# Modulation's sum over partitions: block transposes and row sums on VectorE and four small matmuls in place of 16 TensorE transposes

## The reference

```
mod = silu(c) @ w_mod + b_mod                 # 2048 -> 6 x 2048
sh1, sc1, g1, sh2, sc2, g2 = split(mod, 6)
h = rmsnorm(x, g) * (1 + sc1) + sh1 ; x = x + g1 * attention(h)
h = rmsnorm(x, g) * (1 + sc2) + sh2 ; x = x + g2 * ffn(h)
```

## Time and profile before

| | |
|---|---|
| median of 3 runs | 2319.56 us (2314.96 to 2319.98) |
| profiled execution | 2319.4 us, of which the span from first to last instruction is 2317.5 |
| TensorE, VectorE, ScalarE, GpSimd busy | 2222.8, 1506.3, 1005.4, 15.5 us |
| mean granted TensorE clock | 0.983 of full speed |
| the six sums: transposes (L1507), 96 | 13.2 us busy |
| reductions (L893), 12 | 14.1 us busy |

### The profile page before, as it was taken

One profiled execution on the slowest core, in us unless ns is written; L12 is line 12 of the kernel. 1 busy time (PEld: TensorE's weight loads), 2 busy tenths in 40 slices (PEclk: granted clock), 3 DMA queues, 4 the chain that ended last, 5 costly groups with the idle time before them and its releaser, 6 DMA issues.

```text
span 2317.5 us, 29464 instructions
## 1 busy us (share of the span) xinstructions
PE 2222.8 (96%) x11498; PEld 1901.7 (82%) x11498; DVE 1506.3 (65%) x1417; ACT 1005.4 (43%) x1249; POOL 15.5 (1%) x39
## 2 busy tenths in 40 slices
PE   7999989999999999999999798999999999999997
PEld 6888778788888888888878697787888888888886
DVE  6666455787677767777777864557555655655655
ACT  5443163544344334334354543535443443443442
POOL 0000000000000000000000000000000000000000
PEclk9999999999999999999999899999999999999999
DMA  8775505867877877878867263155656556656553
GB/s 317 285 283 168 162 1 222 283 230 294 290 277 261 307 264 258 310 254 290 294 231 290 91 200 124 74 199 146 194 188 197 185 188 195 189 193 186 181 199 125
DMA packets 213106, 499.67 MB, mean 216 GB/s; under 512 B 10068, under 2 KB 12680, under 8 KB 199800
## 3 DMA queue, kind: packets, MB, share of 16 engines
q1 hardware_dynamic: 211528, 491.16, 61.9%
q0 software_dynamic: 1456, 6.72, 0.8%
HBM read 495.68 MB, written 2.17 MB: 215 GB/s over the span
## 4 chain that ended last, share of the span: by engine, by line
PE 58%; issue 36%; DVE 3%; ACT 1%; DMA 1%; SPq 0%; POOL 0%; DVEq 0%; ACTq 0%; POOLq 0%
PE ps L1443 17%; PE ps L1432 9%; PE ps L1433 9%; PE ps L1434 9%; PE ps L1448 9%; PE ps L1612 2%; ACT prob L665 1%; PE ps L1490 1%; PE ps L1618 1%; DMA raw<-in_nsa_w_in_dram 1%; PE ps L1666 1%; DVE stat L1171 0%; PE ps L1543 0%; DVE h L1036 0%; PE ps L1507 0%
## 5 line engine op out<-in xcount | busy, mean ns | idle before, releaser
L866 DVE TENSOR_TENSOR lower<-raw,upper 128x1024 fp32r<-128x1024 f32 (+1 forms) x733 | 884.2, 1215 | 540.8 <-ACT upper L491 538.1
L491 ACT ACTIVATE upper<-raw 128x1024 fp32r<-128x1024 f32 (+1 forms) x733 | 769.8, 1055 | 974.1 <-PE ps L1434 540.7
L1443 PE MATMUL ps<-xs,upper 128*128 128x512 f32 x2688 | 677.4, 394 | 6.4 <-DVE h L956 4.5
L1443 PEld LDWEIGHTS ps<-xs,upper 128*128 128x128 f32 x2688 | 485.2, 190 | 95.7 <-issue 6.7
L1432 PE MATMUL ps<-upper,hidden 128*128 128x512 f32 x1024 | 399.2, 390 | 0.2 <-DVE lower L866 0.2
L1433 PE MATMUL ps<-lower,hidden 128*128 128x512 f32 x1024 | 398.5, 389 | 0.0
L1434 PE MATMUL ps<-upper,hidden 128*128 128x512 f32 x1024 | 398.4, 389 | 0.0
L1448 PEld LDWEIGHTS ps<-xs,lower 128*128 128x128 f32 x2688 | 367.5, 191 | 26.3
L1448 PE MATMUL ps<-xs,lower 128*128 128x256 f32 x2688 | 375.6, 283 | 0.0
L1432 PEld LDWEIGHTS ps<-upper,hidden 128*128 128x128 f32 x1024 | 192.2, 188 | 40.8 <-DVE lower L866 1.4
L1434 PEld LDWEIGHTS ps<-upper,hidden 128*128 128x128 f32 x1024 | 192.2, 188 | 40.4
(11 more groups left out here) (243 smaller groups left out, 1176.1 us busy)
## 6 DMA issues: line engine op xcount, KB each, us to landing
raw<-in_ffn_w_dram SPq DMA_DIRECT2D x128, 1024.0 KB, 5.9
raw<-in_w_ff_dram SPq DMA_DIRECT2D x128, 1024.0 KB, 5.3
modraw<-in_w_mod_dram SPq DMA_DIRECT2D x96, 1024.0 KB, 7.8
raw<-in_nsa_w_in_dram SPq DMA_DIRECT2D x40, 1024.0 KB, 5.2
raw<-in_nsa_w_out_dram SPq DMA_DIRECT2D x16, 1024.0 KB, 7.4
raw<-in_ple_w_gate_dram SPq DMA_DIRECT2D x16, 1024.0 KB, 5.2
raw<-in_w_out_dram SPq DMA_DIRECT2D x16, 1024.0 KB, 5.1
raw<-in_w_in_dram SPq DMA_DIRECT2D x12, 1024.0 KB, 5.3
```

Of the source, the lines that this page charges most:

```text
L491: nc.scalar.activation(dst, src, ACT.Copy).then_inc(upper_ready, 1)
L866: nc.vector.tensor_tensor(low, src, up, ALU.subtract).then_inc(lower_ready, 1)
L1443: mm(ps[:, 4 * par + f, :], up[:, kk, f * P:(f + 1) * P], both, start=(k == 0), stop=False, skip_group_check=True)
```

## The change

`fold_mod`, new, runs on VectorE: it transposes `modacc` in 32x32 blocks into `modfold` and sums every 32 columns, so that `modsum` [128, 64] holds at partition 32 r + j the sum over a quarter of the partitions. TensorE then adds the four quarters by four matmuls with `quads` (four 32x32 identities stacked, [128, 32]), each of 16 columns into 32 partitions of one bank. VectorE adds the bias from PSUM (16 columns). The order changes too: fold_mod stands at s = 3, TensorE's part behind step 5 instead of step 1, store_mod at s = 6 ahead of the second add_mod. The bias table's matmul stays behind step 1.

```diff
+            nc.gpsimd.memset(quads[:], 0.0)
...
+            for r in range(4):
+                sel = nc.gpsimd.affine_select(out=quads[:], in_=quads[:], compare_op=ALU.not_equal, fill=1.0,
+                                              base=-32 * r, pattern=[[-1, 32]], channel_multiplier=1)
+                if r < 3:
+                    link(sel)
...
+            def fold_mod():
+
+                dve.wait_ge(mod_added, c.at(mod_added))
+                link(nc.vector.transpose(modfold[:], modacc[:]))
+                nc.vector.tensor_reduce(modsum[:], modfold[:].rearrange("p (c i) -> p c i", i=32), AX.X,
+                                        ALU.add).then_inc(mod_folded, 1)
+
             def store_mod(m):
...
-                for i, bank in enumerate((2, 6)):
-                    op = nc.vector.tensor_reduce(modsum[:, i], ps[:, bank:bank + 2, :].rearrange("p b (k n) -> p (b k) n", n=P),
-                                                 AX.X, ALU.add)
-                link(op)
-                nc.vector.tensor_tensor(dst, modsum[:].rearrange("p a k -> p (a k)"), b, ALU.add).then_inc(mod_stored, 1)
+                nc.vector.tensor_tensor(dst, ps[:, 2, 0:KC], b, ALU.add).then_inc(mod_stored, 1)
...
                     if s == 3 and store is not None:
+                        fold_mod()
+                    if s == 6 and store is not None:
                         store_mod(store)
                     if mods is not None and s in at:
                         add_mod(mods + (s == at[1]))
...
+            fold_mod()
             store_mod(5)
...
-            def sum_mod(wait, before=-1):
-
-                pe.wait_ge(mod_added, wait)
+            def sum_mod(folded, before=-1):
+
+                pe.wait_ge(mod_folded, folded)
                 pe.wait_ge(evacuated, c.at("groups", before))
-                for k in range(KC):
-                    op = nc.tensor.transpose(ps[:, (2, 3, 6, 7)[k // 4], k % 4 * P:(k % 4 + 1) * P],
-                                             modacc[:, k * P:(k + 1) * P], ident[:])
+                for r in range(4):
+                    op = mm(ps[32 * r:32 * r + 32, 2, 0:KC], quads[:], modsum[:].rearrange("p (k r) -> p r k", r=4)[:, r, :],
+                            start=True, stop=True)
                 op.then_inc(mod_summed, 1)
...
-            def sums_and_bias():
-                sum_mod(KC)
-
+            def bias_by_bucket():
+                pe.wait_ge(evacuated, c.at("groups", -1))
                 pe.wait_ge(aux_landed, 16 * 5)
                 mm(ps[0:SWA_HEADS, 4, 0:P], relb[:], onehot[:], start=True, stop=True).then_inc(bias_sum, 1)
...
-            group(tokens, xs, between={1: sums_and_bias})
+            group(tokens, xs, between={1: bias_by_bucket, 5: lambda: sum_mod(1)})
...
-                    group(tokens, hidden, ready=ready, between={1: between} if between and g == 0 else None)
+                    group(tokens, hidden, ready=ready, between={5: between} if between and g == 0 else None)
```

More of the change, by code:

```diff
@@ L125, in program @@
         probT = place("probT", [P, 2, 12 * P], at=M + 12288)
+        modfold = place("modfold", [P, D], at=U + 32768)
         blk = place("blk", [P, CMP_LEN, NSA_G, N_CMP], at=G)
@@ L170, in program @@
         modcol = place("modcol", [P, 6, KC])
-        modsum = place("modsum", [P, 2, KC // 2])
+        modsum = place("modsum", [P, D // 32])
+        quads = place("quads", [P, 32])
         silu_c = place("silu_c", [P, KC])
@@ L204, in program @@
         mod_landed = [sem(f"mod_landed{i}") for i in range(2)]
-        mod_added, mod_summed, mod_stored = sem("mod_added"), sem("mod_summed"), sem("mod_stored")
+        mod_added, mod_folded, mod_summed, mod_stored = sem("mod_added"), sem("mod_folded"), sem("mod_summed"), sem("mod_stored")
         x_landed = [sem(f"x_landed{i}") for i in range(T)]
@@ L1728, in between @@
                     sum_mod(c.at("mods", 0))
-                    c.next("mods", KC)
+                    c.next("mods")
                 if modulated:
-                    c.n["mods"] = 2 * KC
+                    c.n["mods"] = 2
                 quarter(norms, between if modulated else None)
@@ L1734, in ffn @@
                 if modulated:
-                    per["mods"] = KC
+                    per["mods"] = 1
                 with loop(pe, c, QUARTERS - 1, per):
@@ L1752, in _ @@
             pe.wait_ge(evacuated, c.at("groups"))
-            sum_mod(6 * KC, 0)
+            sum_mod(6, 0)
             pe.wait_ge(mod_stored, 6)
```

## The result

The changed kernel takes 2328.52 us, the median of 6 runs (2324.51 to 2331.16), against 2319.77 for the kernel before (6 runs): a ratio of 1.0039, 95% interval 1.0027 to 1.0052. That is 8.75 us slower. The forecast was 14 us slower, with a range from 2321 to 2343. Of the eleven executions of a later kernel, the one with both orders, one took 7873.84 us and is left out of its ratio.

What follows compares the result with a forecast made beforehand. TensorE was taken as the bound where five of six sums are made. Terms: −1.2 first sum, +8.9 network, +3.9 last sum, +2.5 clock, together +14.1 us, giving 2333.5 us, range 2321 to 2343.

Steps and rivals of the forecast that it cites:

- the loop's three sums: Feed-forward loop's three trips: each sum costs 4.5 us in place of 1.75 + 0.4, +2.3 us each, +6.9 together.
- the last sum: At 1304 us, TensorE idle: fold, matmuls at half clock and store take 6.2 us in place of 2.35, +3.9 us.
- the clock term: Stalls of 2.2 us can lower TensorE's clock; one or two of four counted: +2.5 us, from nothing to +6.8.
- What TensorE saves: Per sum, 16 transposes costing 1.75 us give way to four matmuls costing 0.6: 1.15 us saved where nothing else moves.
- The nearest rows: Profile rows used to price TensorE's four new matmuls: at most 1.04 us for eight records, the middle, 0.5 us, taken.
- The fold's length: VectorE's block transpose and reduction at 2.35 us each: 4.7 us, or 4.74 with the semaphore between them.
- the 2.35 us row: Profile row of VectorE's second add, two tensors read; its pace was taken for both the transpose and the reduction.
- The 1.28 us row: Profile row of VectorE's first add, one tensor; the lower end for each new operation, making the fold 2.6 us.
- The first stall: TensorE waits ahead of step 4, since the fold runs ahead of split 4: 2.2 us, in the loop 2.3.
- The second stall: TensorE waits ahead of step 7: store_mod's wait at s = 6 holds up split 7, 1.0 us, in the loop 1.6.
- the late step 4: In the kernel before, step 4 of the loop's trips starts late behind a 0.21 us pause; counted as 0.4 us.
- The first sum: At 206 us: VectorE's earlier wait hides the fold and no add follows, so the saving stays, −1.2 us.

Runs made afterwards that it cites:

- both orders: Changed kernel with, in the feed-forward network, the fold behind split 4, the first add behind split 5 and store_mod behind split 7: 2314.14 us, ratio 0.9974 to the kernel before.
- the later store: Changed kernel with store_mod behind split 7 in the feed-forward network, instead of ahead of the second add and split 7: 2324.83 us, ratio 1.0023 to the kernel before.
- the early last fold: Changed kernel with the last section's fold ahead of the final norm, into a tile of its own: 2325.06 us, ratio 1.0028 to the kernel before.
- The kernels with 56 and 80 records: 56: the last section on TensorE, 2310.00 us. 80: both orders plus unused transposes, 16 in each of five sums (2329.21 us) or 48 in an idle stretch (2322.23 us).
- the last section on TensorE: Both orders, and for section 5 TensorE multiplies the unfolded sum with a column of ones instead of a fold: 2310.00 us, ratio 0.9960 to the kernel before.
- 48 transposes more: Both orders plus unused TensorE transposes: 16 in each of the first five sums, 2329.21 us, or 48 in the idle stretch at the first block's end, 2322.23 us.

## Why the prediction was right

The direction, the size to within its range, and both stalls in the network were right. The terms for the loop's three sums and for the last sum were too large, two were missing, and the clock term stood in the wrong place: that its size came out near the forecast is luck. The budget below splits the spans at the starts of the same ScalarE instructions (the 330th, 640th, 800th, 1000th and 1240th of 1249) and takes the means of two profiles of each kernel. The two profiles of the kernel before differ by 4.3 us in the first row and by up to 1.8 us in the others, so a row says no more than that.

| stretch | before | changed | difference |
|---|---|---|---|
| start to the first network, with the first sum | 470.2 | 469.0 | −1.2 |
| first network and embedding, four sums | 733.35 | 743.35 | +10.0 |
| gate's product to the second block's attention, last sum | 243.35 | 245.1 | +1.75 |
| attention and output | 250.1 | 250.0 | −0.1 |
| second network | 596.8 | 594.75 | −2.05 |
| rest | 24.55 | 25.1 | +0.55 |
| span | 2318.3 | 2327.3 | +9.0 |

- **What TensorE saves.** 1.75 us go, as read; putting them back cost 1.73. The four matmuls put off the next step by 0.28 us and slow the matmuls behind them by 0.15: 0.43 us where the forecast had 0.6. Their eight records stand within 0.26 us in the timeline. The nearest rows had a stationary of 128 columns, and I took half their price. The Trainium skill ("TensorEngine Tiling (Array Packing)", Tiling Modes and Performance Considerations) says that a stationary of 32 columns lets four column tiles of the array work at once; the trace agrees, with eight records of 0.2 us in 0.26 us.
- **The fold's length.** 4.63 us against 4.74 forecast. For the reduction the Trainium skill ("VectorE: DVE Perf Modes", the perf-mode tier table) lists the slowest mode even for fp32 from SBUF. The trace agrees: 2.29 us, the pace of the 2.35 us row. The 1.28 us row was the wrong neighbour for both operations.
- **The first stall.** Forecast 2.2 and 2.3 us, measured 2.12 from start to start (1.96 to 2.04 in the bracket). The two experiments that shorten or move the fold show its cause.
- **The second stall.** Forecast 1.0 and, in the loop, 1.6; measured pauses are 0.74 and 1.02, which from start to start are 0.16 more. The store's registers cost 0.3 us in the loop and not the 0.6 of the earlier trace rows.
- **A sum in the network.** Forecast +2.0 for the first and +2.3 for each trip. From its first matmul to the next group's first one, the group took 23.55, 24.13, 23.85 and 23.88 us before and takes 25.57, 25.89, 25.87 and 25.87 us: +2.0, +1.8, +2.0 and +2.0, 7.8 us in place of 8.9. The first was right. In the loop the second stall was 0.4 us too large, and of the kernel before I took the late step 4 of one trip for all three.
- **The first sum.** Its fold was hidden, as forecast. Its group took 24.09 us and takes 22.76, −1.3 us where −1.2 was forecast. Another 0.5 us went in the next group, where TensorE's wait for VectorE (tile `hid`, near 238 us) is 0.79 us in place of 1.29; no term had that.
- **The last sum.** Forecast +3.9, measured +2.7. The step that failed here is the price at half clock, 1.3 us for eight records and their latency. They took 0.31 us in all and the store began 0.37 us after their start.
- **The clock.** Forecast: one or two of the four stalls of 2.2 us bring it down, +2.5 us. In four profiles with these stalls (the changed kernel twice, the later store, the early last fold) one stall of sixteen did. Half clock at the loop's turns came 1.5 times more per profile than before; at 1.7 us each that is 2.5 us, and the first network grew by 2.2 beyond its four sums. That the change caused it is not shown. The stretch after such a pause, granted clock in the seventh column:

```profile
825.00:828.00 3.00, 0.60 (x3) 0.52 (x4) 3.00 (x3) 0.96 (x1) 0.00 (x0) 0.99 0.87 299
828.00:831.40 3.40, 3.40 (x12) 2.83 (x11) 1.62 (x1) 0.00 (x0) 0.00 (x0) 0.51 0.80 228
```

- **What I had not counted.** The second network got 2.05 us faster, untouched, since the pauses at its turns went. The kernels with 56 and 80 records of sums in place of 32 bring pauses back, and with 56 the stretch is 1.2 us longer, so such pauses follow the length of TensorE's code ahead of the loop.

The terms as measured are −1.3 − 0.5 + 7.8 + 2.7 = +8.7 us; the clock adds about 2.2 at the first network's turns and the code's place takes 2.05. That gives 8.9 of the 9.0 us between the spans. That it fits so well is partly chance: the first row is uncertain by more than 1 us, and the row of the last sum shows 1.75 for its 2.7, since one profile of the kernel before has 3.4 us at half clock at 1202 us that the other three lack.

## What to carry to other kernels

An engine that is idle a third of the time can have no slack at the one place where the work is put: read the margin there, from the due time of the next thing it delivers, and put the new work behind that thing. A wait in an in-order queue costs what stands behind it, so a store that nobody needs soon belongs behind the split that somebody does. When a change alters a program's length, look also at stretches that it does not touch before its effect is called shown.

## What the runs showed of the hardware

- The start of TensorE's matmuls where a loop turns depends on the code ahead of the loop. At the second network's two turns the pauses were 0.5 to 1.1 us in the kernel before, under 0.25 us in the changed one, 0.33 and 0.78 us with the last section on TensorE, and 2.1 to 2.35 us with 48 transposes more, wherever these stood. Each pause ended 1.25 to 2.09 us behind a 16 KB packet of the instruction queue; that TensorE waits for this code is likely and not shown.
- Four fp32 matmuls with a 32-column stationary, 16 columns and outputs in four partition quarters take 0.26 us together, and 0.31 us at the 1.2 GHz level.
- A transpose in 32x32 blocks of 128x2048 fp32 takes 2.305 us, a row sum over as much 2.286 us.
- Pauses of 2.0 to 2.6 us at the first network's loop turns were followed by 3.4 us at 1.2 GHz in 14 of 26 cases (13 profiles), pauses of 2.0 us ahead of step 4 in 1 of 16, and pauses of 2.1 to 2.35 us at the second network's turns in 3 of 4. What tells them apart stays open.
